# Experts: scatter places of all 32 experts found once per layer, routing weights worked out at the 13th expert, loops written out

## The reference

```python
def hier_moe(x, wg, bg, we, be, w1, w3, w2):
    ...
    g_sel = jnp.argmax(g_logits, axis=-1)
    ...
    top_v, top_i = lax.top_k(e_logits, TOP_K_IN_GROUP)
    weights = (jax.nn.softmax(top_v, axis=-1) * g_prob[:, None]).reshape(-1)
    ...
    def expert_block(args):
        xi, e = args
        hid = jax.nn.silu(xi @ w1[e]) * (xi @ w3[e])
        return hid @ w2[e]
    ...
    y = jax.ops.segment_sum(yb * slot_w[:, None], slot_tok, num_segments=t + 1)[:t]
```

## Time and profile before

| | |
|---|---|
| time, median of 3 runs | 1748.03 us (1746.92 to 1750.51) |
| time of the profiled execution | 1745.22 us |
| its span | 1743.4 us |
| TensorE busy | 1552.1 us, 89% of the span, 8414 products |
| VectorE, ScalarE, GpSimd busy | 452.7, 296.7, 145.3 us |
| moved by DMA | 522.14 MB, 299 GB/s on average |
| expert stages | about 418 to 900 us and 1224 to 1708 us |

### The profile page before, as it was taken

How to read it: one execution, slowest core, us unless ns; L and a number is a source line. 1 busy time by engine, 2 the same in 40 slices (tenths; PEclk the granted TensorE clock), 3 DMA queues, 4 the chain that set the end, 5 groups by cost and what they waited for, 6 DMA issues and landing times.

```text
span 1743.4 us, 21453 instructions
## 1 busy us (share of the span) xinstructions
PE 1552.1 (89%) x8414; PEld 740.9 (42%) x8414; DVE 452.7 (26%) x1063; ACT 296.7 (17%) x597; POOL 145.3 (8%) x199
## 2 busy tenths in 40 slices
PE   4899877797999999999967998796999999999991
PEld 3445765444344444334423444444434443334440
DVE  0212275623311111111113023633311111111113
ACT  1100112511111111111112003521111111111112
POOL 1101103000000000000014000010000000000000
PEclk9899977797999999999987998997899999999996
DMA  9977954014999999999979422023599999999992
GB/s 348 259 262 268 330 203 163 7 70 179 419 423 423 423 423 423 424 424 424 423 285 300 168 99 85 1 77 133 203 421 424 424 423 423 424 425 422 424 387 112
DMA packets 99382, 522.14 MB, mean 299 GB/s; under 512 B 10090, under 2 KB 11562, under 8 KB 56320
## 3 DMA queue, kind: packets, MB, share of 16 engines
q1 hardware_dynamic: 85920, 485.58, 68.9%
q0 software_dynamic: 13408, 35.81, 6.5%
HBM read 511.60 MB, written 20.22 MB: 305 GB/s over the span
## 4 chain that ended last, share of the span: by engine, by line
PE 83%; DVE 9%; DMA 3%; ACT 2%; issue 1%; SPq 1%; POOL 0%; DVEq 0%; POOLq 0%; ACTq 0%
PE psum L831 25%; PE psum L519 14%; PE psum L844 13%; PE psum L812 10%; PE psum L777 5%; PE psum L837 3%; PE psum L824 2%; PE psum L818 2%; PE psum L462 2%; DMA ring<-in_ada_w 1%; PE psum L787 1%; PE psum L705 1%; PE psum L692 1%; DVE area_q L1219 1%; DVE small L1229 1%
## 5 line engine op out<-in xcount | busy, mean ns | idle before, releaser
L831 PE MATMUL psum<-ring,area_t 128*64 128x512 f32 x1024 | 451.8, 594 | 2.9 <-issue 1.2
L832 PE MATMUL psum<-ring,area_t 128*64 128x512 f32 x1024 | 452.1, 595 | 0.0
L831 PEld LDWEIGHTS psum<-ring,area_t 128*64 128x64 f32 x1024 | 139.8, 137 | 293.9 <-issue 292.7
L519 PE MATMUL psum<-ring,area_t 128*128 128x512 f32 (+1 forms) x576 | 242.5, 583 | 0.0
L844 PE MATMUL psum<-ring,area_t 128*64 128x512 f32 x1024 | 233.9, 599 | 2.2 <-DVE area_t L1704 2.2
L1675 DVE COPY area_q<-psum 64x512 f32<-64x512 f32 x64 | 44.5, 695 | 573.4 <-PE psum L832 573.3
L812 PE MATMUL psum<-area_h,area_t 128*64 128x512 f32 x768 | 181.1, 607 | 3.0 <-DVE area_t L1689 3.0
L519 PEld LDWEIGHTS psum<-ring,area_t 128*128 128x128 f32 x576 | 110.3, 193 | 128.1 <-issue 126.3
L1881 POOL DMA_INDIRECT pair_rows<-area_q,idx x64 | 62.3, 973 | 941.2 <-ACT area_q L1137 926.6
L832 PEld LDWEIGHTS psum<-ring,area_t 128*64 128x64 f32 x1024 | 140.0, 138 | 0.0
L844 PEld LDWEIGHTS psum<-ring,area_t 128*64 128x64 f32 x1024 | 68.2, 136 | 119.3 <-issue 111.8
(11 more groups left out here) (242 smaller groups left out, 1303.6 us busy)
## 6 DMA issues: line engine op xcount, KB each, us to landing
ring<-in_moe_w SPq DMA_DIRECT2D x192, 2048.0 KB, 16.0
ring<-in_ada_w SPq DMA_DIRECT2D x24, 2048.0 KB, 16.5
ring<-in_na_w_in SPq DMA_DIRECT2D x6, 2048.0 KB, 18.5
ring<-in_ab_w_in SPq DMA_DIRECT2D x5, 2048.0 KB, 11.0
area_m<-mod_ready POOLq DMA_DIRECT2D x6, 1024.0 KB, 9.5
area_q<-pair_rows POOLq DMA_DIRECT2D x6, 1024.0 KB, 7.0
ring<-in_ab_w_out SPq DMA_DIRECT2D x2, 2048.0 KB, 15.3
area_g<-mod_ready POOLq DMA_DIRECT2D x4, 1024.0 KB, 7.9
```

The lines of the kernel that those rows point to most:

```text
L519: mm = pe.matmul(banks[2 + g % 4][:, 0:w], hT[:, k, t * P:t * P + P], wchunk(n, KT)[:, k, 0:w], start=(k == 0), stop=(k == KT - 1))
L831: pe.matmul(banks[2 + u][0:64, :], lhsT, w1[:, k, :], start=(k == 0), stop=(k == KT - 1))
L832: mm = pe.matmul(banks[2 + u][64:128, :], lhsT, w3[:, k, :], start=(k == 0), stop=(k == KT - 1))
```

## The change

- The two choices of a token get their slots once per layer. New `rank_slots` on VectorE, after the first `tokens` copy, makes for each choice k a one-hot matrix `slots[:, k]` (token to slot, from the token's rank) and a table `val[k]` (token by expert, with the row number of the pair). New `places` on TensorE multiplies the two, six products with 32 columns, in expert 0 between the turns of expert 1's tokens and expert 0's down products. New `index` on VectorE turns the result into one table `idx` of 128 slots by 32 experts. The scatter of expert e takes column e of it.
- The index products, the index operation and the waits between them are gone from every expert; `pick` waits for `tok_done` of two experts before, not for `index_done`, and compares 64 slots per tile, not 128.
- `weigh` stands after expert 12 (`WEIGH_AT`), not after expert 0.
- The loops over experts on SyncE, TensorE, ScalarE and VectorE are written out, and wait for constants.
- The `val` product and the two `pval` additions leave `route`; they are in `rank_slots`.

```diff
+        WEIGH_AT = 12
...
+                for e in range(EXPERTS):
                     for j in range(3):
-                        at = place(base + 3 * u + j)
-                        dst = expert_dst(ring[:, at, :], j)
-                        if isinstance(e, int) and e < 2:
-                            freed(sp, base + 3 * e + j - RING)
-                        else:
-
-                            sp.wait_ge(M["y_done"] if j == 2 else M["hid_done"], e + (l * EXPERTS - 1))
-                        sp.dma_start(dst, expert_dram(l, e, j)).then_inc(landed[at], 16)
-
-                one(0, 0)
-                one(1, 1)
-                with sp.Fori(1, EXPERTS // 2) as i:
-                    for u in range(2):
-                        one(sp.snap(i * 2 + u), u)
+                        n = NUM["moe", l, 3 * e + j]
+                        load(n, expert_dst(ring[:, place(n), :], j), expert_dram(l, e, j))
...
-            def turn_tokens(e, u, base):
-
-                if not (isinstance(e, int) and e + base < 1):
-                    pe.wait_ge(M["index_ready"], e + base)
-                column = [val[:, t, e:e + 1] if isinstance(e, int) else val[:, t, bass.ds(e, 1)] for t in range(NT)]
-                index_products([(sel[u][:, t, :], column[t]) for t in range(NT)]).then_inc(M["index_done"], 1)
-                pe.wait_ge(M["tok_copied"], e + (base + 1))
-                if not (isinstance(e, int) and e + base < 1):
-                    pe.wait_ge(M["xT_copied"], e + base)
+            def turn_tokens(l, e):
+                E = l * EXPERTS + e
+                pe.wait_ge(M["tok_copied"], E + 1)
+                if E >= 1:
+                    pe.wait_ge(M["xT_copied"], E)
                 token_turns().then_inc(M["xT_done"], 1)
 
-            def hidden(e, u, base, w1, w3):
-                pe.wait_ge(M["xT_copied"], e + (base + 1))
-                if not (isinstance(e, int) and e + base < 2):
-                    pe.wait_ge(M["silu_done"], e + (base - 1))
-                    pe.wait_ge(M["up_copied"], e + (base - 1))
+            def places(l):
+
+                pe.wait_ge(S["slots_ready"], l + 1)
+                for k in range(2):
+                    for t in range(NT):
+                        mm = pe.matmul(banks[5][:, 0:EXPERTS], slots[:, k, t, :], val[k][:, t, :],
+                                       start=(k == 0 and t == 0), stop=(k == 1 and t == NT - 1))
+                mm.then_inc(S["places_done"], 1)
...
-                with pe.Fori(1, EXPERTS // 2 - 1) as i:
-                    for u in range(2):
-                        one(pe.snap(i * 2 + u), u, False)
-                one(EXPERTS - 2, 0, False)
-                one(EXPERTS - 1, 1, True)
+                tokens(l, 0)
+                turn_tokens(l, 0)
+                for e in range(EXPERTS):
+                    ns = [NUM["moe", l, 3 * e + j] for j in range(3)]
+                    ws = [wchunk(ns[j], 4 if j == 2 else KT) for j in range(3)]
+                    for j in range(2):
+                        pe.wait_ge(landed[place(ns[j])], when(ns[j]))
+                    hidden(l, e, ws[0], ws[1])
+                    if e + 1 < EXPERTS:
+                        tokens(l, e + 1)
+                    turn_hidden(l, e)
+                    if e + 1 < EXPERTS:
+                        turn_tokens(l, e + 1)
+                    if e == 0:
+                        places(l)
+                    pe.wait_ge(landed[place(ns[2])], when(ns[2]))
+                    down(l, e, ws[2])
...
-                stt(val, o2, 2.0, last(keep[:, KEEP["pair"]], EXPERTS), ALU.mult, ALU.add)
-                for k in range(2):
-                    ts(pval[:, k, :], keep[:, KEEP["pair"]], 2.0 * k, None, ALU.add)
-
                 v.wait_ge(S["ranks_done"], l + 1)
                 tt(sl, banks[2][:, 0:96].rearrange("p (t n) -> p t n", t=NT), chosen, ALU.mult)
                 cp(cnt, banks[2][:, 96:128])
                 ts(key, sl, -1.0, None, ALU.add, name="chosen_keys")
+
+            def rank_slots(l):
+
+                for k, (oh, rank) in enumerate(((o1, m1), (o2, m2))):
+                    ts(pval[:, k, :], keep[:, KEEP["pair"]], 2.0 * k, None, ALU.add)
+                    tt(val[k], oh, last(pval[:, k, :], EXPERTS), ALU.mult)
+                    tt(c32, oh, key, ALU.mult)
+                    red(rank, c32, ALU.add)
+                    tt(slots[:, k, :, :], lead(keep[:, KEEP["slot"]], NT), last(rank, P), ALU.is_equal,
+                       "dve_step" if k == 0 else "slots_ready")
...
-            def pick(e, u, base):
-
-                if not (isinstance(e, int) and e < 2):
-
-                    v.wait_ge(M["index_done"], e + (base - 1))
-                rank = key[:, :, e] if isinstance(e, int) else key[:, :, bass.ds(e, 1)].rearrange("p t e -> p (t e)")
-                v.tensor_tensor(sel[u], lead(keep[:, KEEP["slot"]], NT), last(rank, P), ALU.is_equal)\
-                    .then_inc(M["sel_ready"], 1)
-
-            def index(e, u, base):
-
-                v.wait_ge(M["index_done"], e + (base + 1))
-                if not (isinstance(e, int) and e + base < 2):
-                    v.wait_ge(M[f"scattered{u}"], scat(e, u, base) - 16)
-                v.tensor_scalar(idx[u][:, :], banks[5][:, 0:1], keep[:, KEEP["skip"]], None, ALU.add)\
-                    .then_inc(M["index_ready"], 1)
...
+            def pick(l, e):
+                u, E = e % 2, l * EXPERTS + e
+                if e >= 2:
+                    v.wait_ge(M["tok_done"], E - 1)
+                v.tensor_tensor(sel[u][:, :, 0:BLOCK], lead(keep[:, KEEP["slot"]][:, 0:BLOCK], NT),
+                                last(key[:, :, e], BLOCK), ALU.is_equal).then_inc(M["sel_ready"], 1)
+
+            def index(l):
+
+                v.wait_ge(S["places_done"], l + 1)
+                do(v.tensor_scalar(idx[:, :], banks[5][:, 0:EXPERTS], keep[:, KEEP["skip"]], None, ALU.add),
+                   "places_ready")
...
-                def whole(e, u, lasts=2):
-                    one(e, u, base)
-                    product(e, u, base)
-                    if lasts:
-                        tokens(e + 1, 1 - u, base)
-                        index(e + 1, 1 - u, base)
-                    if lasts > 1:
-                        pick(e + 2, u, base)
-
-                pick(0, 0, base)
-                pick(1, 1, base)
-                tokens(0, 0, base)
-                index(0, 0, base)
-                whole(0, 0)
-                weigh(l)
-                whole(1, 1)
-                with v.Fori(1, EXPERTS // 2 - 1) as i:
-                    for u in range(2):
-                        whole(v.snap(i * 2 + u), u)
-                whole(EXPERTS - 2, 0, 1)
-                whole(EXPERTS - 1, 1, 0)
+                pick(l, 0)
+                pick(l, 1)
+                tokens(l, 0)
+                rank_slots(l)
+                for e in range(EXPERTS):
+                    one(l, e)
+                    product(l, e)
+                    if e + 1 < EXPERTS:
+                        tokens(l, e + 1)
+                    if e + 2 < EXPERTS:
+                        pick(l, e + 2)
+                    if e == 0:
+                        index(l)
+                    if e == WEIGH_AT:
+                        weigh(l)
...
+                pool.wait_ge(S["places_ready"], l + 1)
                 for e in range(EXPERTS):
-                    scatter(M, e, e % 2, base, l)
+                    scatter(M, e, e % 2, base, l, idx[:, e:e + 1])
```

More of the change, by code:

```diff
@@ L236, in build @@
         eid_i = sb("eid_i", [P, OVER + 1], I32)
-        idx = [sb(f"idx{u}", [P, 1], U32) for u in range(2)]
+        idx = cond32[:, 0, :].bitcast(U32)
+        idx_over = sb("idx_over", [P, 1], U32)
         landed = [sem(f"weights_landed{i}") for i in range(RING)]
@@ L896, in one @@
-                def one(e, u, last):
-                    ws = [wchunk(start + 3 * u + j, 4 if j == 2 else KT) for j in range(3)]
-                    wait_chunk(e, u, 0)
-                    wait_chunk(e, u, 1)
-                    hidden(e, u, base, ws[0], ws[1])
-                    if not last:
-                        tokens(e + 1, 1 - u, base)
-                    turn_hidden(e, u, base)
-                    if last:
-                        pe.wait_ge(M["index_ready"], e + (base + 1))
-                    else:
-                        turn_tokens(e + 1, 1 - u, base)
-                    wait_chunk(e, u, 2)
-                    down(e, u, base, ws[2])
@@ L1700, in product, with one @@
-            def product(e, u, base):
-                v.wait_ge(M["upT_copied"], e + (base + 1))
-                if not (isinstance(e, int) and e + base < 2):
-                    v.wait_ge(M["y_done"], e + (base - 1))
+            def one(l, e):
+                u, E = e % 2, l * EXPERTS + e
+                v.wait_ge(M["hid_done"], E + 1)
+                if E >= 2:
+                    v.wait_ge(M["hidT_done"], E - 1)
```

(1 more changed line is left out.)

139 lines of the change are left out of this document (63 added, 76 removed).

## The result

The changed kernel takes 1757.12 us (median of 5 runs, 1753.87 to 1762.72), the kernel before 1748.03 (5 runs, 1745.42 to 1750.51). The ratio is 1.0057, with an interval of 1.0033 to 1.0082: slower by 6 to 14 us. The profiled execution took 1757.69 us, with a span of 1755.8, 12.4 more than before.

The account below looks back on a forecast made before the run. The weight stream was taken to bound the expert stages. First pick -0.17 and code packets +0.88 gave +0.7 us a layer by the stream, +1.4 for two layers, so 1748.03 + 1.4 = 1749.4 us, range 1744 to 1766.

Parts of the forecast that it names:

- The forecast's own case: Whole kernel: the summed terms hold, likeliest 1749.4 us, own range 1746.5 to 1753 us, chance 58%.
- the dry start: Rival, stage start: later places work and code packets empty the load queue, +5.5 us, 1753.5 us, chance 8%.
- half of the packets on one engine: Milder form of the 20% rival, weight stream: half the instruction packets meet weights on one DMA engine, 1762 to 1766 us.
- Two candidates for the bound, and the stream wins near the end: Expert stages: TensorE takes 14.84 us an expert, the weight stream 15.20, so a stage ends on the stream.
- Index products gone: the 0.59 us become a wait: Each expert: TensorE waits for VectorE's multiplication instead; 0 gain, +0.02 us an expert on TensorE.
- Slots under the first hidden products, pick, loops as such: Stage start and loops: slots hidden, 0; smaller first pick -0.17 us a layer; loop form itself 0.
- Places: down products of expert 0 later: Expert 0 on TensorE: six products take 1.46 us, so its down products come 1.05 us later.
- I take the stream as unharmed: Stage start: queued loads cover the places delay, 0; other bound, the stream moves by the whole 1.05 us.
- Code: Written-out TensorE loop: some 13.3 to 13.8 more instruction packets a layer, about 28 in all, through the DMA engines.
- I take the even spread: Weight stream: extra instruction packets spread over all 16 DMA engines, costing 0.88 us a layer.
- one engine: Rival, weight stream: all packets on one DMA engine, 14 to 18 us a layer, 1776 to 1784 us, chance 20%.
- Routing weights at the 13th expert: VectorE behind expert 12: the moved block of some 8.2 us stays hidden, cost 0.

Follow-up runs that it names:

- Light loads: Only the first half of each w2 chunk loaded, in the kernel before and in the changed kernel: ratios 0.9964 and 0.9945 to the kernel before.
- light_after: The changed kernel with only the first half of each w2 chunk loaded: ratio 0.9945 to the kernel before.
- rolled_places: The changed kernel with its expert loops put back and the routing-weights block after expert 0: ratio 1.0012 to the kernel before.
- unroll_pe: The kernel before with only TensorE's expert loop written out: ratio 1.0032 to the kernel before.
- rolled_gaps: Like rolled_places, but slots made before the first token copy and places products split over two TensorE gaps: ratio 1.0005 to the kernel before.
- gaps_unroll: The changed kernel with slots made before the first token copy and places products in two TensorE gaps: ratio 1.0009 to the kernel before.
- half_gaps: Like rolled_gaps, but w1 and w3 of expert 2 loaded in halves, the first halves earlier: ratio 0.9992 to the kernel before.
- unroll_all: The kernel before with only the expert loops on all four engines written out: ratio 1.0038 to the kernel before.
- weigh_first: The changed kernel with the routing-weights block back after expert 0 (`WEIGH_AT = 0`): ratio 1.0017 to the kernel before.
- split_unroll: The kernel before with each hidden product issued as two of 256 columns and TensorE's loop written out: ratio 1.0045 to the kernel before.

## Why the prediction was right, and what in it was not

The measured 1757.12 us lies in the range of 1744 to 1766, on the slower side, which had 0.38. The likeliest time, 1749.4, was 7.7 us too low; the direction of the sum (+1.4) was right and its size was not. The forecast's own case, 1746.5 to 1753, doesn't hold the measured time, nor does a rival name it: the dry start alone gives 1753.5, half of the packets on one engine 1762 to 1766. It is the width that the rivals gave the range, not the sum, that has it inside, and in that the range was lucky.

- *Two candidates for the bound, and the stream wins near the end.* Right. Light loads make TensorE the only bound (445.16 us for 30 experts, 14.84 each), and the change is then a gain: 1.9 us over the 30 experts of the first layer, and 1.9 us in the medians, which is not clear of noise.
- *Index products gone: the 0.59 us become a wait.* Right in mechanism, a little off in size. The handover from VectorE to the down products was read at 0.23 us in an idle stretch; in the stream of experts it is 501.64 - 501.57 = 0.07 us to the first weights, the row that the 0.23 came from, and 0.11 us to the first product. So TensorE gains 0.10 us an expert where -0.02 was taken. As predicted, it reaches the end of no stage.
- *Slots under the first hidden products, pick, loops as such.* The two first picks take 0.63 us in place of 1.03, so 0.2 us for the first (0.17 forecast). Loops: light_after has them written out at 14.74 us an expert as rolled_places has with loops, and unroll_pe at 14.84 as the kernel before, so neither gain nor loss on TensorE.
- *Places: down products of expert 0 later.* The changed kernel's timeline in expert 0:

```profile
439.98 0.74 PE L820 MATMUL psum<-keep,area_q 128*128 128x128 f32 x4
...
441.31 1.42 PE L850 MATMUL psum<-area_q 128*128 128x32 f32 x12
...
442.67 3.65 PE L827 MATMUL psum<-ring,area_t 128*64 128x512 f32 x16
```

  1.42 us (1.46 forecast), and 2.69 us from the hidden turns to the down products where it was 1.82: 0.87 us later (1.05 forecast). "I take the stream as unharmed" may have been the wrong end of that bound. Moving the places out of expert 0 goes with streams that are shorter by 0.9 and 1.8 us (rolled_places to rolled_gaps) and by 1.2 and 0.5 us (changed kernel to gaps_unroll); each is within the scatter, all four point the same way, and half_gaps shows that TensorE can hold the stream there. This is the rival of the dry start, a small one, and not shown.
- *Code.* 28 more packets were forecast and came: 66 for 38. The term that was mis-sized is their price: "I take the even spread", 0.88 us a layer; writing out TensorE's loop costs 1.9 and 4.4 us of stream in the two layers (unroll_pe), 2.6 and 4.0 (unroll_all), so about 3.2 a layer. It is neither the even spread (0.06 us a packet) nor one engine (1.02 or more), but 0.2 us. How it goes is seen at single packets. The changed kernel, first the two chunks issued at 446.4 and 453.2, then the instruction queue from 462 to 463:

```profile
L371 SPq DMA_DIRECT2D ring<-in_moe_w x2: 340/354/368, 446.4 to 453.2; - x2
...
DMA to landing us min/median/max: 9.9/10.0/10.0
```

```profile
q8 instruction: 1, 0.02, 5.9%
```

  They land at 456.3 and 463.2, 6.9 us apart and not some 5.1, with a packet at 462; part of that may be the short queue. But of the packets after it in that stage only the one at 684 is followed by a chunk a microsecond late, and one at 898 behind the last w3; the others (491, 520, 549, ..., 867) by chunks at their usual distance or up to 0.6 us late. In the second stage six are followed by a late chunk. So single late chunks alone don't make up the 2.8 us of the first stage, where the kernel before has two as well.

  That it is the packets is seen over all kernels of the table. Take the time from one w3's landing to the next, from expert 7 on; the usual value is 15.16 us. Of 187 such times with a packet on the instruction queue in them, in the six written-out kernels, 22 are more than 0.6 us longer than usual (up to 1.6), 18 are 0.1 to 0.6 us longer, and 147 are not longer. Of 309 without one, in all ten kernels, 9 are 0.1 to 0.6 us longer and none is more. On average a packet adds 0.14 us here (the 0.2 us above have the first experts in them), and most packets add nothing. One reading is that a packet costs its full microsecond when it hits the engine that the others are waiting for, and is hidden otherwise, with packets that go to changing engines. It is argued from landing times and not shown: the trace doesn't name the engine.
- *Routing weights at the 13th expert.* Right by the traces: 0, by streams (914.2 and 914.9 us) and by VectorE's rows; the times of the two kernels differ by more than that, as said above.
- *The rest.* The +0.7 us a layer by the stream is +3.2 a layer in the profiles. That leaves some 3 of the 9.1 us in the medians. The profiled executions have 6.1 us outside the streams, of which 4.2 at the lower clock and in a memory round trip in code that was not changed; this part differs between all kernels, whether their code is written out or not. No run shows that the 3 us of the medians are the same. The Trainium skill (Runtime: NRT & Kernel Launch, Instruction fetch mechanics) calls the cost of crossing to a new block of instructions mostly hidden. Here the trace agrees while the stream has room (light_after). Where the DMA engines are full TensorE itself still doesn't feel it (14.84 us an expert in unroll_pe, as with loops), but the weight stream pays, some 0.2 us a packet.

What stays open: to which engine a packet goes; why gaps_unroll and weigh_first, whose streams (912.5 and 914.9 us) are about as long as those of the other written-out kernels, are 0.1 to 0.2% above the kernel before and those 0.3 to 0.6%; and why the kernel before gains more from light loads than its profiled waits explain. The measured cost of writing out is thus 1 to 7 us by time, and 5 to 8 us by the streams of the profiled executions.

## What to carry to other kernels

Where two resources are within 2% of each other, work taken from one buys at most the distance to the other: follow the growing time to landing before costing a removal. Ask of each removed instruction what was running beside it; here a chain over ScalarE and VectorE let only 0.10 of the 0.59 us through. And a loop written out is not free when the DMA engines are full, since its code comes through them too.

## What the hardware showed that was not expected

TensorE's code arrives in packets on a queue that the other engines' loops leave as it is (unroll_all and unroll_pe both have 69 there), one packet for about 250 to 265 of its records (44 packets for some 11,080 more records in split_unroll, 5 for 1,324 in the earlier trace rows), and one packet holds a DMA engine for 1.0 to 1.1 us (6.4% of 16 engines in 1 us). With the engines full, 31 such packets made two stages of 454 us longer by 6.3 us in all; with a sixth fewer bytes to load, 28 of them cost nothing. Of the 187 landing distances with a packet in them nearly four fifths were no longer than without one. A stream of 2 MB loads that is full later on (share 1.00 to 1.01) was held by its issuer for the first one or two experts: the share was 0.93 there in half_gaps, and 3.4 us of head start shrank to 0.9 and 2.0 us within 28 us.
